# SSD phase: the subtraction of the weight split moves from GpSimd to VectorE, and the squares of y are added up on VectorE before one product with ones

## What is computed

```
proj = h @ w_in
z, xbc, dt_f, dt_b, q_mem = split(proj)
xbc = silu(depthwise_conv_centred(xbc, conv_w, conv_b))
xs, bm, cm = split(xbc)
y = y_fwd + y_bwd + d_skip * xs                  # two chunked scans, 128 tokens a chunk
y = rmsnorm(y * silu(z[..., :2048]), norm_g)     # needs, per token, the sum of y*y over all 2048 channels
x = x + rmsnorm(concat(y, m) @ w_out[0], post_g[0])
```

## Time and profile before

| | |
|---|---|
| timed runs | 2143.32, 2145.84, 2146.58 us; median 2145.84 us |
| profiled execution, first to last instruction | 2143.2 us; the page gives no other time for it |
| TensorE clock granted, mean | 0.997 |
| TensorE busy | 2099.4 us, 98% |
| VectorE busy | 1089.1 us, 51% |
| ScalarE busy | 800.1 us, 37% |
| GpSimd busy | 924.6 us, 43% |

### The profile page before, as it was taken

One profiled execution on the slowest core, in us unless ns is written; L12 is line 12 of the kernel. 1 busy time (PEld: TensorE's weight loads), 2 busy tenths in 40 slices (PEclk: granted clock), 3 DMA queues, 4 the chain that ended last, 5 costly groups with the idle time before them and its releaser, 6 DMA issues.

```text
span 2143.2 us, 31195 instructions
## 1 busy us (share of the span) xinstructions
PE 2099.4 (98%) x12580; PEld 1789.7 (84%) x12580; DVE 1089.1 (51%) x1866; ACT 800.1 (37%) x1943; POOL 924.6 (43%) x623
## 2 busy tenths in 40 slices
PE   8999999999999999999999999999999999999997
PEld 7888887788898888787788887888888888888885
DVE  4104332598898898897712233144333423541447
ACT  4123122465464555473322111143424323432343
POOL 5533332333343343325742332654454445544544
PEclk9999999999999999999999999999999999999999
DMA  5221112335232233235331111322131223123213
GB/s 189 90 68 53 51 50 74 137 98 143 80 109 80 70 118 100 78 119 173 125 125 50 50 50 50 96 87 68 59 88 59 68 59 96 40 68 86 69 50 118
DMA packets 206685, 184.19 MB, mean 86 GB/s; under 512 B 23916, under 2 KB 172684, under 8 KB 206541
## 3 DMA queue, kind: packets, MB, share of 16 engines
q1 hardware_dynamic: 206541, 182.20, 27.7%
HBM read 168.19 MB, written 12.21 MB: 84 GB/s over the span
## 4 chain that ended last, share of the span: by engine, by line
PE 50%; DVE 4%; issue 1%; ACT 0%; DMA 0%; POOL 0%; DVEq 0%; POOLq 0%; ACTq 0%
PE bank L214 25%; PE bank L264 9%; PE bank L574 6%; PE bank L2411 2%; PE bank L2439 2%; PE bank L1067 2%; PE bank L2422 2%; PE bank L1093 1%; DVE acc L944 1%; PE bank L1131 1%; DVE acc L940 1%; DMA R<-macc_dram 0%; PE bank L447 0%; DVE R L422 0%; PE bank L2483 0%
## 5 line engine op out<-in xcount | busy, mean ns | idle before, releaser
L188 POOL TENSOR_SCALAR Wh<-Wraw 128x1024 fp32r<-128x1024 f32 x217 | 245.9, 1133 | 1100.2 <-issue 755.2
L214 PE MATMUL bank<-Hh,Wh 128*128 128x512 f32 (+1 forms) x1936 | 664.6, 343 | 3.2 <-ACT R L817 1.4
L214 PE MATMUL bank<-Hl,Wh 128*128 128x512 f32 (+1 forms) x1936 | 652.0, 337 | 0.0
L214 PE MATMUL bank<-Hh,Wl 128*128 128x512 f32 (+1 forms) x1936 | 651.0, 336 | 0.0
L191 POOL TENSOR_TENSOR Wl<-Wraw,Wh 128x1024 fp32r<-128x1024 f32 x217 | 550.6, 2537 | 18.1
L214 PEld LDWEIGHTS bank<-Hh,Wh 128*128 128x128 f32 x1936 | 367.7, 190 | 51.0 <-issue 10.8
L214 PEld LDWEIGHTS bank<-Hh,Wl 128*128 128x128 f32 x1936 | 367.3, 190 | 39.0
L214 PEld LDWEIGHTS bank<-Hl,Wh 128*128 128x128 f32 x1936 | 367.9, 190 | 36.6 <-issue 1.7
L298 DVE TENSOR_TENSOR acc<-bank,acc 128x512 f32<-128x512 f32 x240 | 165.0, 690 | 166.3 <-PE bank L264 165.5
L264 PE MATMUL bank<-Wh,Mh 128*128 128x512 f32 x528 | 208.7, 395 | 8.7 <-DVE acc L298 7.6
L264 PE MATMUL bank<-Wh,Ml 128*128 128x512 f32 x528 | 205.7, 390 | 0.0
(11 more groups left out here) (259 smaller groups left out, 3124.0 us busy)
## 6 DMA issues: line engine op xcount, KB each, us to landing
Wraw<-in_na_w_in_dram SPq DMA_DIRECT2D x80, 512.0 KB, 3.8
Wraw<-in_ssd_w_in_dram SPq DMA_DIRECT2D x57, 512.0 KB, 4.2
Wraw<-in_w_out_dram SPq DMA_DIRECT2D x48, 512.0 KB, 3.3
R<-acs_dram SPq DMA_DIRECT2D x16, 1536.0 KB, 6.8
Wraw<-in_w_mem_kv_dram SPq DMA_DIRECT2D x32, 512.0 KB, 3.9
R<-gs_dram SPq DMA_DIRECT2D x32, 128.0 KB, 3.5
R<-R SPq DMA_DIRECT2D x32, 128.0 KB, 3.6
macc_dram<-acc SPq DMA_DIRECT2D x1, 3072.0 KB, 11.5
```

The lines of the kernel that those rows point to most:

```text
L188: pool.tensor_scalar(Wh[:, s, :], Wraw[:, s, :], 1.0, 1.0, ALU.mult, ALU.mult).then_inc(pool_c, 1)
L214: mm = pe.matmul(DB[h.k % 2][:, 0:t1 - t0], w[:, k, :], x[:, k, t0:t1], start=(k == 0 and i == 0), stop=(k == KC - 1 and i == 2))
```

## The change

GpSimd's work in the phase is parted in two. For units 6 to 52 it only rounds (`high_unit`, with the semaphore `high_split`); VectorE makes Wl (`low_unit`), at places written into its list: two for pair 0 (units 6 and 7) after the carries; in pairs 1 to 14 one inside `segment`; one before `backward` where the pair has a group unit or output units; one after the carries in the even pairs 2 to 12; one among the additions of those pairs; one at the end of the odd pairs, before the group's taps. Units 4, 5 and 53 on are split by GpSimd as before.

The squares of pair 0 go to a new buffer `pre.sq`; those of pairs 1 to 14 are added to it by VectorE after `segment` of the next pair, and the product with ones is run once at the end, over `pre.sq` and the last pair's squares, into six columns.

```
+        def high_unit(pool):
+            u = U["pool"]
+            s = u.k % 2
+            pool.wait_ge(raw_landed[s], u.base * 8 + 16 * (u.k // 2 + 1))
+            pool.wait_ge(unit_done, u.value + 1)
+            settle(pool)
+            pool.tensor_scalar(Wh[:, s, :], Wraw[:, s, :], 1.0, 1.0, ALU.mult, ALU.mult).then_inc(high_split, 1)
+            u.next()
+
+        def low_unit(dve):
+            u, highs = U["low"], U["high"]
+            s = u.k % 2
+            highs.next()
+            dve.wait_ge(high_split, highs.value)
+            dve.wait_ge(w_ready, u.value + 2)
+            dve.tensor_tensor(Wl[:, s, :], Wraw[:, s, :], Wh[:, s, :].bitcast(F32), ALU.subtract).then_inc(w_ready, 1)
...
+            FIRST_LOW, END_LOW = 6, unit_index(LAST) - 1
...
-                for _ in range(unit_index(PAIRS) - 4 + 2):
-                    split_unit(pool)
+                for u in range(4, unit_index(PAIRS) + 2):
+                    if FIRST_LOW <= u < END_LOW:
+                        high_unit(pool)
+                    else:
+                        if u == END_LOW:
+                            pool.wait_ge(w_ready, U["pool"].value + 2)
+                        split_unit(pool)
...
-                        if n:
-                            act.wait_ge(sq_summed, n)
+                        if n > 1:
+                            act.wait_ge(sq_summed, n - 1)
                         take_spans(act, z, ACT.Silu)
...
-                        act.activation(z, y, ACT.Square).then_inc(sq_done, 1)
+                        act.activation(z if n else pre.sq, y, ACT.Square).then_inc(sq_done, 1)
...
+                        if 0 < n < LAST:
+                            low_unit(dve)
                         dve.tensor_tensor(seg, seg, ab[:, 1, :, :].rearrange("p h (c l) -> p c h l", l=P), ALU.min)\
                             .then_inc(seg_ready, 1)
 
                     segment()
+                    if n > 1:
+                        dve.wait_ge(sq_done, n)
+                        if n > 2:
+                            dve.wait_ge(sq_summed, n - 2)
+                        dve.tensor_tensor(pre.sq, pre.sq, z, ALU.add).then_inc(sq_summed, 1)
...
+                    if n and group_unit(n) or out_in(n):
+                        low_unit(dve)
 
                     backward(n)
...
+                    if out_in(n) and n < LAST - 1:
+                        low_unit(dve)
...
+                            def then(k):
+                                tap(j, n + 1, 2 * half + k)
+                                if (half, k) == (1, 0):
+                                    low_unit(dve)
...
                         if n:
                             low_part(n - 1)
+                        for _ in range(2 if n == 0 else 1):
+                            low_unit(dve)
                     for kind, group in group_units(n):
                         conv5(j + 1, conv_row(kind, group), dense + (1 if n else 2))
...
-                        dve.tensor_reduce(ssum, A[0][:, 256:256 + PAIRS * NT].rearrange("p (n i) -> p i n", i=NT), AXX,
-                                          ALU.add).then_inc(reduced, 1)
+                        dve.tensor_copy(ssum, A[0][:, 256:256 + NT]).then_inc(reduced, 1)
...
-                def squares(n, signal=sq_summed):
-                    pe.wait_ge(sq_done, n + 1)
+                def squares():
+                    pe.wait_ge(sq_done, PAIRS)
+                    pe.wait_ge(sq_summed, LAST - 1)
                     for i in range(NT):
-                        mm = pe.matmul(A[0][:, 256 + n * NT + i:257 + n * NT + i], z[:, i * P:(i + 1) * P],
-                                       ones[:, 0:1], start=True, stop=True)
-                    mm.then_inc(signal, 1)
+                        for k, sq in enumerate((pre.sq, z)):
+                            mm = pe.matmul(A[0][:, 256 + i:257 + i], sq[:, i * P:(i + 1) * P], ones[:, 0:1],
+                                           start=(k == 0), stop=(k == 1))
+                    mm.then_inc(summed, 1)
...
-                    if 0 < n < LAST:
-                        squares(n - 1)
```

More of the change, by code:

```diff
@@ L139, in encoder_kernel @@
         raw_landed = [sem("raw_landed0"), sem("raw_landed1")]
-        w_ready, unit_done = sem("w_ready"), sem("unit_done")
+        w_ready, unit_done, high_split = sem("w_ready"), sem("unit_done"), sem("high_split")
         half_done, dense_free = sem("half_done"), sem("dense_free")
@@ L145, in encoder_kernel @@
         dve_c, act_c, pool_c = sem("dve_c"), sem("act_c"), sem("pool_c")
-        U = {k: Count() for k in ("sp", "pool", "pe", "act", "dve")}
+        U = {k: Count() for k in ("sp", "pool", "pe", "act", "dve", "low", "high")}
         HF, HD = ({k: Count() for k in ("pe", "act", "dve")} for _ in range(2))
@@ L1176, in window @@
                 at, r.at = r.at, 0
-                self.ab, self.cs, self.xx, self.spare = r(2, 2, T), r(2, 2, 4, P), r(3, NT, P), r(2 * PAIRS)
+                self.ab, self.cs, self.xx, self.sq, self.spare = r(2, 2, T), r(2, 2, 4, P), r(3, NT, P), r(T), r(2 * PAIRS)
+                assert r.at <= at
                 r.at = at
@@ L1730, in vector @@
                 dve.wait_ge(pre.cst[2], 32)
+                U["low"].k = unit0 + FIRST_LOW
                 def low_part(n):
@@ L1848, in vector @@
                         for half in range(2):
-                            dve_out(dve, (half,), first=(n == 2), then=lambda k: tap(j, n + 1, 2 * half + k) if n < LAST else None)
+                            def then(k):
+                                tap(j, n + 1, 2 * half + k)
+                                if (half, k) == (1, 0):
+                                    low_unit(dve)
+                            dve_out(dve, (half,), first=(n == 2), then=then)
                     elif n < LAST:
@@ L1886, in vector @@
                     if half == 0:
-                        dve.tensor_reduce(ssum, A[0][:, 256:256 + PAIRS * NT].rearrange("p (n i) -> p i n", i=NT), AXX,
-                                          ALU.add).then_inc(reduced, 1)
+                        dve.tensor_copy(ssum, A[0][:, 256:256 + NT]).then_inc(reduced, 1)
+                assert U["low"].k == unit0 + END_LOW
                 HF["dve"].k = half0 + 2 * dense_index(PAIRS)
@@ L1934, in tensor @@
                     g, a = n // 4, n % 2
[L1936 to L1941, removed]
-                            squares(n - 1)
-                        pe_dense(pe, between=between)
+                    pe_dense(pe, between=lambda: turn_x(n))
                     pe.wait_ge(x_scaled, n + 1)
@@ L1994, in tensor @@
                         if half == k == 0:
-                            squares(LAST, summed)
+                            squares()
                         nxt.mem_norm.pe(pe, 2 * half + k)
```

## The result

| | before | after |
|---|---|---|
| timed runs, median (range) | 2143.32 (2141.87 to 2146.58), 5 runs | 2194.17 (2193.66 to 2195.47), 5 runs |
| profiled execution: own time; span | 2143.32; 2143.2 | 2194.22; 2192.2 |
| TensorE busy; granted clock, mean | 2099.4; 0.997 | 2103.0; 0.986 |
| idle of TensorE (span less busy) | 43.8 | 89.2 |

The ratio is 1.0233, 95% interval 1.022 to 1.0245: 50.9 us slower. Slower was forecast, but by 24.9 us; 2194 lies outside the range of 2146 to 2184. Nothing was changed ahead of the phase.

What follows compares the result with a forecast made beforehand. TensorE and VectorE were each taken as the bound for part of the cycle, with 0.25 us slack at the hand-over. The terms summed to 24.9 us on 2143.2, set on the median 2170.7 us; range 2146 to 2184.

Steps and rivals of the forecast that it cites:

- The first addition in pairs 3 to 10: VectorE's first output addition comes 2.7 us later in each of four double pairs, 10.8 us together.
- From the first addition on everything shifts together: Behind VectorE's first output addition in a double pair, all later work shifts by the same delay, with no further cost.
- TensorE's gain is spent in waiting: Over two pairs output tiles start 2.6 us earlier, but the third still waits for VectorE's first addition.
- Pair 0: Unit 6 waits for VectorE's carries, starts 7.0 us late, and a net 4.8 us passes to pair 1.
- Pair 1: VectorE waits 3 us at unit 10, whose weights land late; y is delayed 1.2 us more.
- Pair 2: Three subtractions, added squares and two roundings, less 3.1 us lost now, cost 2.9 us, with no slack.
- Pairs 11 and 12: Five subtractions up to the first addition, where 8 to 9 us are lost now, cost 1.6 us.
- Pairs 13 and 14: Four subtractions there cost 2.0 us.
- Pair 15 and the tail: 0.88 us more before the carries and 24 last product records instead of 12, half under waits, cost 1.6 us.
- The dearer one: Rival, 15%: roundings at 1.05 us, subtractions at 1.2, one or two more waits of 3 us each; 2183 us.
- No change: Rival, 10%: roundings fall beside VectorE work that reads PSUM and cost nothing; 2143 us.
- faster: Rival, 10%: roundings free, subtractions 0.88 us, TensorE keeps all its 17.6 us less 4.8 at the start; 2133 us.

Runs made afterwards that it cites:

- no_squares: Changed kernel with GpSimd splitting every unit whole and VectorE's additions of squares left out, so sums cover pairs 0 and 15 alone: 2158.92 us, ratio 1.0062.
- warm: Changed kernel with 18 products of no use (36 records) put into TensorE's wait for the first addition in pairs 2 to 12: 2182.67 us, ratio 1.0176.
- lows_only: Changed kernel with the squares handled as before (products with ones in every pair), the subtractions staying on VectorE: 2161.79 us, ratio 1.0071.
- out_low_on_pool: Changed kernel with GpSimd splitting whole the six units whose subtraction VectorE makes among the output additions: 2184.95 us, ratio 1.018.
- pair0_on_pool: Changed kernel with GpSimd splitting units 6 and 7 whole: 2186.02 us, ratio 1.0183.
- no_squares_hold: As no_squares, with GpSimd's split of the unit of x(n+1) in pairs 3, 5, 7 and 9 held until VectorE finished `backward`: 2158.26 us, ratio 1.0064.

## Why the prediction was right in its sign and wrong in its size

*What bounds the kernel: right.* VectorE's stretch up to the first output addition sets the pace. The output tiles wait 4.4 to 4.8 us for it (forecast: 5), and TensorE's shorter list gains nothing.

*The first addition in pairs 3 to 10: right.* For pairs 5 and 6 the balance on VectorE was +3.0 us and measured +2.61; in pairs 3 and 4 the addition was to come 2.7 late and comes 2.8. The subtraction costs 1.14 from start to start (616.00 to 617.14; forecast 1.15). The added squares take 1.72 (618.81 to 620.53) and not 0.88, since a rounding lies beside them, by GpSimd's timeline of the stretch:

```profile
618.12 1.68 POOL L201 TENSOR_SCALAR Wh<-Wraw 128x1024 fp32r<-128x1024 f32 x1 [11.37 <-PE bank L232]
628.24 1.19 POOL L201 TENSOR_SCALAR Wh<-Wraw 128x1024 fp32r<-128x1024 f32 x1 [8.44 <-PE bank L232]
```

That is 0.84 for the rounding, the price taken; the second one costs `backward` 0.79 (4.02 instead of 3.23). All five roundings before the first addition cost 3.9 us (forecast 4.2). The rule of the Trainium skill (SBUF — State Buffer, "Who interferes with whom"), by which a rounding blocks for its whole length, would make each 1.05; here the rows stay under it. For a train of small instructions under a whole split the rule is nearer: `backward` lost 3.0 us to passes of 3.5 us in `no_squares`.

*"From the first addition on everything shifts together": this is the step that failed.* Forecast 0, measured +2.39 in pairs 5 and 6. The balance stopped at the first addition. Two things behind it have a price. One is the granted clock, 0.5 to 0.6 behind the wait: 3.6 us at 0.53 lose 1.7, 3.4 us at 0.63 lose 1.3. The other is the subtraction among the later additions, which I had counted in no term of its own: the second output unit waits 0.86 us for it (680.28). Two runs part them. VectorE's first addition of pair 6 and the start of pair 7, in `warm` and then in `lows_only`:

```profile
661.38 1.28 DVE L316 TENSOR_TENSOR acc<-bank,acc 128x512 f32<-128x512 f32 x2
...
684.20 1.82 DVE L1795 TENSOR_TENSOR R<-bank,R 128x512 f32<-128x512 f32 x2 [1.46 <-PE bank L1967]
```

```profile
658.53 1.28 DVE L316 TENSOR_TENSOR acc<-bank,acc 128x512 f32<-128x512 f32 x2
...
681.30 1.82 DVE L1795 TENSOR_TENSOR R<-bank,R 128x512 f32<-128x512 f32 x2 [1.46 <-PE bank L1963]
```

The stretch is 22.03 us before and 24.42 after. With the wait filled (`warm`) it is 22.82, so 1.6 of the 2.39 is the price of the wait; with the subtraction but a wait of only 0.5 us (`lows_only`) it is 22.77, so 0.7 to 0.8 is the subtraction. The other three double pairs show the same: 1.3 to 1.5 and 0.6 to 0.8. `out_low_on_pool`, which takes this subtraction away, is no clean measure of it: its first wait stays (4.4 and 4.8 us), the clock behind it is lower still (0.50 for 4.0 us in three of the four), and in the four double pairs it wins only 2.1 us; the rest of its 9.7 lies in pairs 2 and 11 to 15. The four double pairs 3 to 10 so cost 19.8 us (5.0, 5.0, 4.9, 4.9) instead of 10.8; pairs 5 and 6 last 77.8 us, forecast 75.5. "TensorE's gain is spent in waiting" was true and too cheap: the waiting has a price of its own, and `warm` got 11.5 us of it back. A rule of the Trainium skill (TensorE: Matmul & The Clock Gate, "HAM oscillation — how this bites in real kernels") says that a kernel whose TensorE waits between bursts falls back to the low clock, and that the loss is the time at that level times one half. The trace agrees: 0.50 to 0.63 behind waits of 4.4 to 7.8 us, and 22 us of TensorE's busy time in the phase beyond its work.

*Pair 0: the delay right, the end not.* Forecast were carries that end at 436.0 and unit 6 at 437.2; on that axis they end at 436.1 and it starts at 437.4 (433.3 and 434.56 on the axis of after). The end of the carries was met by two errors that cancel: `backward` fell to 4.02 us and not to 3.23, and the taps in front of it from 4.88 to 4.18, which the forecast left out. VectorE's timeline from there:

```profile
433.29 2.55 DVE L210 TENSOR_TENSOR Wl<-Wraw,Wh 128x1024 fp32r<-128x1024 f32 x2
446.27 4.20 DVE L1348 SCALAR_TENSOR_TENSOR R<-R 128x770 f32<-128x770 f32 x4 [10.44 <-ACT R L1287]
```

The taps start at 449.1 on the axis of before, 2.0 later than forecast, because the unit's first 4.0 us run at a clock of 0.50. The term was 4.8 and measured 6.8. In `pair0_on_pool` VectorE begins pair 1 7.8 us earlier than in after (33.4 us behind the start of pair 0 instead of 41.2), and the whole phase is 7.1 us shorter: the price arises in pair 0 and is carried to the end. The 10 us by the excess hold 2 us of difference between the two sessions.

*Pair 1: right.* Forecast were a wait of 3 us for late weights and a term of 1.2 us. The term measured 0.8, and VectorE waits 3.05 us:

```profile
478.11 1.23 DVE L210 TENSOR_TENSOR Wl<-Wraw,Wh 128x1024 fp32r<-128x1024 f32 x1 [3.05 <-issue]
```

*Pair 2:* forecast 2.9, measured 6.4. This pair has output units too, and I gave it neither the clock nor the second wait; with the wait filled (`warm`) it costs 3.6. *Pairs 11 and 12:* forecast 1.6, measured 4.5: 1.8 up to the first addition, 2.6 behind it. *Pairs 13 and 14:* forecast 2.0, measured 6.9 by TensorE's transposes: the subtraction of unit 50 came too late for TensorE, 3.63 us (945.20), a wait that the walk did not have. *Pair 15 and the tail:* forecast 1.6, measured 4.6, with a wait of 3.4 us for the carries (L2018 in the waits above; 1.6 before). Together the phase has 24.9 us more than forecast: 9.0 in the four double pairs, 4.9, 3.5, 3.0, 2.9 and 2.0 in the others, less 0.4 in pair 1. Some 2 us behind the phase have a source that stays open.

*The rivals.* The dearer one had more or longer waits, but not the clock, and stopped at 2183. "No change" and "faster" needed free roundings; `no_squares` shows that with the splits left where they were TensorE's gain does not come through even without any addition.

*What stays open.* In `no_squares` the slower clock (13.4) and the idle time beyond the work saved (20.2 less 17.6) share the loss; how much of the idle time the new collisions make was not separated, since holding GpSimd's pass back only moved it. The clock is not a plain matter of one wait's length: in `no_squares` the products behind a wait of 2.44 us ran at 1.00, in `no_squares_hold` behind one of 2.43 us at 0.59. The first row is the wait in `no_squares`, where 654.20 to 658.20 had a clock of 1.00; the second is the window of `no_squares_hold`, in which its wait ends at 647.84.

```profile
654.20 0.50 PE L284 MATMUL bank<-Wh,Mh 128*128 128x512 f32 x1 [2.44 <-DVE acc L318]
```

```profile
647.50:651.50 4.00, 3.66 (x9) 2.92 (x10) 2.50 (x4) 1.68 (x6) 0.24 (x1) 0.59 0.47 131
```

## What to carry to other kernels

Where two engines take turns as the bound, find the hand-over and count each engine's work up to it; an engine that is made faster ahead of a hand-over only waits, and a long wait of TensorE then also costs clock on the work behind it, 1.3 to 2 us behind each wait of 4.4 us or more whose window is shown here. Price the stretch behind the hand-over as well, and every small thing placed in it. Work between VectorE and GpSimd is moved unit by unit: what collides with VectorE's two-input work goes to VectorE, what falls beside its idle time or ahead of a waiting TensorE stays (19 units moved gained 6.3 us, 47 lost 16.7). That the choice of the 19 and not their smaller number makes the gain was not tested with another set.

## What the runs showed of the hardware that was not expected

- The lower TensorE clock comes back in the middle of a busy kernel: 0.50 for 4 us behind a wait of 7.8 us, 0.53 to 0.63 for about 3.5 us behind waits of 4.4 and 4.8.
- Products of no use paid: 25 us of them, in waits, made the kernel 11.5 us faster.
- Contention reached GpSimd as well: the 47 roundings inside the phase took 1.48 us in the mean, the other 170 took 1.08.
- Taking 17.6 us of work off the engine that is 98% busy made the kernel 13.7 us slower (`no_squares`): TensorE was idle 20.2 us more and busy 13.4 us longer than its work took. A new collision of GpSimd's passes with `backward` is seen; its share is not.
